# Four of the twelve modulation units move from TensorE to VectorE, and their weights are loaded earlier

## The reference, cut to what matters

```python
mod = jax.nn.silu(c) @ w_ada[l] + b_ada[l]
shift1, scale1, gate1, shift2, scale2, gate2 = jnp.split(mod, N_MOD, axis=-1)
h = modulate(rmsnorm(x, norm1_w[l]), shift1, scale1)      # needs shift1, scale1
...
x = x + gate1[:, None, :] * mix                           # after the mixers
h2 = modulate(rmsnorm(x, norm2_w[l]), shift2, scale2)     # before the experts
...
x = x + gate2[:, None, :] * ffn
```

## Time and profile before

| what | value |
|---|---|
| median of three runs | 918.78 us (916.0 to 918.87) |
| the profiled execution | 919.4 us, of which the span is 917.6 us |
| PE, DVE, ACT, POOL busy | 97%, 45%, 34%, 12% of the span |
| mean rate of the loads | 314 GB/s |
| 0 to 245 us | everything ahead of the experts |

### The profile page before, as it was taken

One profiled execution on the slowest core, in us unless ns is written; L12 is line 12 of the kernel. 1 busy time (PEld: TensorE's weight loads), 2 busy tenths in 40 slices (PEclk: granted clock), 3 DMA queues, 4 the chain that ended last, 5 costly groups with the idle time before them and its releaser, 6 DMA issues.

```text
span 917.6 us, 13421 instructions
## 1 busy us (share of the span) xinstructions
PE 893.3 (97%) x5530; PEld 575.9 (63%) x5530; DVE 410.6 (45%) x697; ACT 314.3 (34%) x507; POOL 106.2 (12%) x116
## 2 busy tenths in 40 slices
PE   5999999999999999999999999999998999999998
PEld 2688876777644434444344444444435899999886
DVE  2357725368522323222223232223234778888643
ACT  1227335342522222322222212222213555555531
POOL 1024463031000000000000000000000022222200
PEclk9999999999999999999999999999999999999999
DMA  9962259787999899999999999999999665555301
GB/s 353 415 291 93 93 193 355 282 326 292 398 402 419 313 420 421 421 419 420 420 421 418 419 421 420 423 419 419 421 421 357 217 194 183 180 179 184 128 1 47
DMA packets 60892, 289.47 MB, mean 315 GB/s; under 512 B 4500, under 2 KB 28692, under 8 KB 33688
## 3 DMA queue, kind: packets, MB, share of 16 engines
q1 hardware_dynamic: 59104, 284.13, 78.3%
q10 hardware_dynamic: 1720, 4.40, 1.2%
HBM read 287.47 MB, written 1.05 MB: 314 GB/s over the span
## 4 chain that ended last, share of the span: by engine, by line
PE 90%; DVE 3%; DMA 3%; issue 2%; ACT 1%; POOL 1%; SPq 0%; ACTq 0%; DVEq 0%
PE ps L1032 24%; PE ps L1056 12%; PE ps L537 8%; PE ps L1020 7%; PE ps L1153 7%; PE ps L1154 7%; PE ps L1155 7%; PE ps L620 4%; PE ps L1072 3%; PE ps L1045 2%; DMA ring<-in_ada_units_dram 2%; PE ps L552 2%; PE ps L520 2%; DMA S<-in_first_cols_dram 1%; PE ps L511 1%
## 5 line engine op out<-in xcount | busy, mean ns | idle before, releaser
L1035 PE MATMUL ps<-ring,proj 128*64 128x512 f32 x320 | 140.9, 593 | 0.0
L1032 PE MATMUL ps<-ring,proj 128*64 128x512 f32 x304 | 133.9, 593 | 0.0
L1853 DVE TENSOR_TENSOR w_l<-ring,w_h 128x2048 fp32r<-128x2048 f32 x33 | 75.5, 2292 | 44.8 <-ACT w_h L2201 44.8
L1153 PE MATMUL ps<-h_h,w_h 128*128 128x256 f32 x336 | 95.1, 283 | 0.0
L1154 PE MATMUL ps<-h_l,w_h 128*128 128x256 f32 x336 | 95.1, 283 | 0.0
L1155 PE MATMUL ps<-h_h,w_l 128*128 128x256 f32 x336 | 95.1, 283 | 0.0
L1032 PEld LDWEIGHTS ps<-ring,proj 128*64 128x64 f32 x304 | 41.1, 137 | 84.6 <-issue 84.6
L1032 PE MATMUL ps<-arena,proj 128*64 128x512 f32 x208 | 91.6, 593 | 0.0
L2201 ACT CAST w_h<-ring 128x2048 fp32r<-128x2048 f32 x33 | 62.8, 1903 | 81.4 <-PE ps L1155 76.9
L1709 DVE SCALAR_TENSOR_TENSOR RQ<-ps,gate_of,proj 128x512 f32<-128x512 f32 x32 | 24.0, 751 | 147.1 <-PE ps L1057 147.1
L2157 ACT CAST MX_r<-RQ 64x512 fp32r<-64x512 f32 x62 | 38.2, 616 | 143.9 <-DVE RQ L1709 143.1
(11 more groups left out here) (372 smaller groups left out, 1601.7 us busy)
## 6 DMA issues: line engine op xcount, KB each, us to landing
ring<-in_w_dram SPq DMA_DIRECT2D x114, 1024.0 KB, 15.0
arena<-in_w_dram SPq DMA_DIRECT2D x72, 1024.0 KB, 15.7
ring<-in_ada_units_dram SPq DMA_DIRECT2D x11, 2048.0 KB, 8.6
ring<-in_ffn_w_in_dram SPq DMA_DIRECT2D x22, 1024.0 KB, 8.1
ring<-in_in_units_dram SPq DMA_DIRECT2D x6, 2048.0 KB, 23.1
ring<-in_ffn_w_out_dram SPq DMA_DIRECT2D x5, 2048.0 KB, 8.0
arena<-in_in_units_dram SPq DMA_DIRECT2D x2, 2048.0 KB, 24.8
ring<-in_out_units_dram SPq DMA_DIRECT2D x2, 2048.0 KB, 9.2
```

Source lines behind the costliest of these rows:

```text
L1032: pe.matmul(ps[0:SLOTS, :], XTe[i % 2][:, k, :], u1[:, k, :], start=(k == 0), stop=(k == 7))
L1035: t = pe.matmul(ps[64:64 + SLOTS, :], XTe[i % 2][:, k, :], u3[:, k, :], start=(k == 0), stop=(k == 7))
L1153: pe.matmul(ps, ah, bh, start=first, stop=False)
L1853: ve.tensor_tensor(low, src, dst.bitcast(F32), ALU.subtract).then_inc(split_ready, 1)
```

## The change

- Units 4 to 7 are no longer made on TensorE. VectorE makes them by a new `ada(j)`: eight instructions over 128 x 512, the first a product of the unit's first 512 columns with a number per partition (`ccol`), the other seven a product with such a number and an addition to the sum so far. Each waits for the one ahead of it. The sum over the partitions is left to the small product on TensorE, now with the constant `ones` in place of `sel`.
- Unit 4 is loaded between units 1 and 0 of the delta projection, and unit 5 between units 0 and 2; before, both came after three `proj` units. VectorE makes them in pieces of two instructions among its convolutions. Units 6 and 7 are made whole, at the ends of VectorE's levels 1 and 2.
- `gate_total(4)` and `(5)` move on TensorE from level 4 to ahead of `project(0)`, and on VectorE from the end of level 3 to ahead of level 1.
- `spread_out` and ScalarE's copies now write contiguously; the stride of eight is in the reading of the weights of `column_total` instead. For segments 3 and 4 (units 6 to 9) eight matmuls with 128 columns of weights take the place of sixteen with 64.
- The slots are dealt out anew: `proj` 0 and 1 now wait for VectorE's units 4 and 5, and later units follow in a rotated order of slots.

```diff
L1256 DVE COPY part<-ps tensor_program
             def gate_total(j, src):
                 ps = take("total", j)
-                pe.wait_ge(*drained("ada", j))
-                pe.matmul(ps[:, :], sel, src, start=True, stop=True).then_inc(*mm.up("total", j))
+                pe.wait_ge(ada_rows, by_vector.index(j) + 1)
+                pe.matmul(ps[:, :], ones, src, start=True, stop=True).then_inc(*mm.up("total", j))
...
             def column_totals(seg):
-                column_total(seg, 1, column_total(seg, 0))
+                ps = take("columns", seg)
+                for half in range(2):
+                    if seg == 3:
+                        pe.wait_ge(ada_rows, by_vector.index(2 * seg + half) + 1)
+                    else:
+                        pe.wait_ge(*drained("ada", 2 * seg + half))
+                for c in range(8):
+                    i = pe.matmul(ps[:, 2 * c:2 * c + 2], by_eights[:, c, :], (ones if seg == 3 else sel)[:, 0:2], start=True, stop=True)
+                i.then_inc(*mm.up("columns", seg, 0))
+                mm.at["columns", seg, 1] = mm.n
...
+            gate_total(4, part[0])
+            gate_total(5, part[1])
             project(0)
             project(1)
...
-                elif level == 5:
-                    ada(7)
                 elif level == 2:
                     project(3)
...
                 elif level == 4:
-                    gate_total(4, part[0])
-                    gate_total(5, part[1])
                     turn_rotated(0)
...
                     project(4)
-                    ada(4)
-                elif level == 3:
-                    ada(5)
                 elif level == 4:
                     turn_rotated(1)
-                    ada(6)
L1256 DVE COPY part<-ps vector_program
+            def ada(j, chunks=range(8)):
+
+                w, dst = unit(("ada", j), 512), part[j % 2]
+                for c in chunks:
+                    if c == 0:
+                        if j in (4, 5):
+                            ve.wait_ge(*mm.of("columns", 1, 1))
+                        else:
+                            ve.wait_ge(*mm.of("total", j - 2))
+                        ve.wait_ge(*filled(("ada", j)))
+                        ve.tensor_scalar(dst, w[:, 0, :], ccol[:, 0:1], None, ALU.mult).then_inc(*vd.up("ada", j))
+                    else:
+                        ve.wait_ge(*vd.of("ada", j))
+                        ve.scalar_tensor_tensor(dst, w[:, c, :], ccol[:, c:c + 1], dst, ALU.mult,
+                                                ALU.add).then_inc(*((ada_rows, 1) if c == 7 else vd.up("ada", j)))
...
-                ve.tensor_copy(by_eights[:, :, 64 * (j % 2):64 * (j % 2) + 64].rearrange("k c p -> k p c"),
-                               full("ada", j)[:, :].rearrange("k (p c) -> k p c", c=8)).then_inc(*free("ada", j))
+                ve.tensor_copy(part[j % 2], full("ada", j)[:, :]).then_inc(*free("ada", j))
...
-            delta_conv(1, range(4))
-            delta_conv(0, range(4))
+            delta_conv(1, range(1))
+            for m in range(1, 4):
+                delta_conv(1, (m,))
+                ada(4, range(2 * m - 2, 2 * m))
+            for m in range(4):
+                delta_conv(0, (m,))
+                ada(4, (6, 7)) if m == 0 else ada(5, range(2 * m - 2, 2 * m))
             ve.tensor_copy(ab_turned, full("ab")[:, 0:256]).then_inc(*free("ab"))
             delta_conv(2, (0,))
+            ada(5, (6, 7))
...
+            gate_total(4)
+            gate_total(5)
             idb = mid(cst("ident_half"), 4)
...
                 if level == 1:
                     lower(3)
+                    ada(6)
                 elif level == 2:
                     lower(5)
-                elif level == 3:
-                    gate_total(4)
-                    gate_total(5)
+                    ada(7)
L1256 DVE COPY part<-ps scalar_program
-                    ada(4)
...
-                    ada(5)
...
-                    ada(6)
                 elif level == 5:
-                    ada(7)
                     higher(6)
L1256 DVE COPY part<-ps sync_program
             load_in("dn", 1, 2560)
+            load_ada(4)
             load_in("dn", 0, 2048)
+            load_ada(5)
             load_in("dn", 2, 3072)
...
             load_in("proj", 1, 512)
-            load_ada(4)
-            load_ada(5)
             load_ada(6)
             load_ada(7)
```

More of the change, by code:

```diff
@@ L289, in program @@
         part = [part_[:, n, :] for n in range(2)]
-        by_eights = part_[:, :, :].rearrange("k a b -> k (a b)").rearrange("k (c p) -> k c p", c=8)
+        by_eights = part_[:, :, :].rearrange("k a b -> k (a b)").rearrange("k (p c) -> k c p", c=8)
         row_high = [v.rearrange("p (k t) -> p k t", k=4) for v in (vrow_r[:, :], gates_r[:, 1, :])]
@@ L409, in program @@
         HIGH, FIFTH = 3, 4
-        for name, s in ((("ada", 0), 0), (("ada", 1), 1), (("ada", 2), 2), (("ada", 3), HIGH), (("dn", 1), R + 1), (("dn", 0), R),
-                        (("dn", 2), FIFTH), (("proj", 2), 0), (("proj", 0), 1), (("proj", 1), 2), (("ada", 4), FIFTH), (("ada", 5), 0),
-                        (("ada", 6), 1), (("ada", 7), FIFTH), (("proj", 3), 2), (("ada", 10), 0), (("ada", 8), 1), (("ada", 9), FIFTH),
-                        (("proj", 4), 0), (("ada", 11), 2), (("wo", 0), 1), (("wo", 1), FIFTH)):
+        for name, s in ((("ada", 0), 0), (("ada", 1), 1), (("ada", 2), 2), (("ada", 3), HIGH), (("dn", 1), R + 1), (("ada", 4), 0),
+                        (("dn", 0), R), (("ada", 5), 1), (("dn", 2), FIFTH), (("proj", 2), 2), (("proj", 0), 0), (("proj", 1), 1),
+                        (("ada", 6), FIFTH), (("ada", 7), 2), (("proj", 3), 0), (("ada", 10), FIFTH), (("ada", 8), 1), (("ada", 9), 2),
+                        (("proj", 4), FIFTH), (("ada", 11), 0), (("wo", 0), 1), (("wo", 1), 2)):
             units.place(name, s)
@@ L434, in program @@
         for i, name in enumerate(moe_order):
-            units.place(name, (2, 0, 5, 6, 7, 1, FIFTH, HIGH)[i % (R + 3)])
+            units.place(name, (0, FIFTH, 5, 6, 7, 1, 2, HIGH)[i % (R + 3)])
         units.place(("mixer",), 1, 2)
         for i, name in enumerate([("fin", u) for u in range(11)] + [("fout", u) for u in range(6)]):
-            units.place(name, (FIFTH, HIGH, 2, 0, 1)[i % R], 2 if name[0] == "fin" else 1)
+            units.place(name, (2, HIGH, 0, FIFTH, 1)[i % R], 2 if name[0] == "fin" else 1)
         first_a, first_b, second_in = sem("first_down_a"), sem("first_down_b"), sem("second_down")
@@ L476, in program @@
         chunk_ready_a, chunk_ready_v = sem("chunk_ready_a"), sem("chunk_ready_v")
-        diagonal_ready = sem("diagonal_ready")
+        diagonal_ready, ada_rows = sem("diagonal_ready"), sem("ada_rows")
+        by_vector = (4, 5, 6, 7)
         rows_made, gated, router_scaled, h2_rows = (sem(n) for n in ("rows_made", "gated", "router_scaled", "h2_rows"))
@@ L794, in tensor_program @@
                     ada(10)
-                else:
+                elif level == 6:
                     project(7)
@@ L1910, in ada @@
                 ps, dst = full("ada", j), part[j % 2]
-                if j in (6, 7):
-                    ac.wait_ge(*mm.of("total", 4))
-                    ac.wait_ge(*mm.of("total", 5))
-                elif j in (4, 5, 8, 9):
-                    ac.wait_ge(*mm.of("columns", {4: 1, 8: 3}[j - j % 2], 1))
+                if j in (8, 9):
+                    ac.wait_ge(*mm.of("columns", 3, 1))
                 elif j > 9:
                     dst = late_part[j % 2]
-                if j in (6, 7, 8, 9):
-                    half = slice(64 * (j % 2), 64 * (j % 2) + 64)
-                    ac.copy(by_eights[:, :, half].rearrange("k c p -> k p c"),
-                            ps[:, :].rearrange("k (p c) -> k p c", c=8)).then_inc(*free("ada", j))
-                else:
-                    ac.copy(dst, ps[:, :]).then_inc(*free("ada", j))
+                ac.copy(dst, ps[:, :]).then_inc(*free("ada", j))
             ac.wait_ge(*vd.of("scale1"))
@@ L2411, in used @@
                 if kind == "ada":
-                    return mm.of("ada", i)
+                    return (ada_rows, by_vector.index(i) + 1) if i in by_vector else mm.of("ada", i)
                 if kind == "dn":
```

## The result

The changed kernel takes 931.25 us, the median of four runs (928.9 to 935.13), beside 918.83 for the kernel before (916.0 to 918.89). The ratio is 1.0141, with an interval of 1.0101 to 1.0182. The forecast was 917.6 us with a range of 913.8 to 920.4, so it had the sign wrong and the range too narrow. The profiled execution took 929.36 us, its span 927.6, 10.0 us more than before.

The account below looks back on a forecast made before the run. TensorE was taken as the bound, busy 893.3 of 917.6 us, with GpSimd deciding at level 4's end. Terms -1.9 + 1.0 - 0.1 - 0.2 gave -1.2: 918.2 us profiled, 917.6 as median, range 913.8 to 920.4.

Parts of the forecast that it names:

- The columns: Contiguous `spread_out` writes and eight 128-column matmuls in `column_totals`: 0.1 us won at the start, 0.2 in all.
- TensorE's clock: One fall from 2.4 to 1.2 GHz expected among the level 5 waits, costing 1.0 us (bounds 0 and 1.9).
- The gate totals: Moved ahead of `project(0)`, they take 1.8 us there; a 0.23 us wait goes, so what follows is 1.6 later.
- Units 4 and 5: On VectorE between convolutions: 5.0 us a unit, 1.3 a pair, fitting its idle time; cost taken as 0.
- Unit 6: On VectorE behind `lower(3)`: 5.0 us fits the 5.87 idle ahead of `lower(4)`; cost 0.
- Unit 7: Behind `lower(5)`, taking turns with GpSimd: `rotate(1, 0)` begins at 137.8 us for 135.21, level 5's mask ready at 147.8.
- Levels 4 and 5: TensorE waits 2.9 us for the last rotated half, 1.0 for the mask, 0.9 for the copy; -1.9 at level 5's `xm`.
- The sum: All terms for the whole kernel: -1.9 + 1.0 - 0.1 - 0.2 = -1.2 us.
- The rival on the slow side: Long waits at level 4's end bring the clock down twice or longer, a turn costs 0.69: +2, 920.8 us; chance 0.11.
- the third case: Rival: GpSimd isn't held up by unit 7, level 5's mask at 145.3: -4.8 us, 914.0; chance 0.17.

Follow-up runs that it names:

- the doubled groups: Kernel before, with its sixteen contiguous small matmuls of `column_totals` for segments 3 and 4 each sent twice over: 922.26 us, ratio 1.0055.

## Why the prediction was wrong

*The columns* is the step that failed: a term of the sum that was put at almost nothing. "with 128 columns of weights they take 0.23 each (...), so eight are again 1.8." The price was read from a row whose weights are read contiguously, and the new reading has a stride of eight. With it the eight take 3.7 us, and 2.08 for 1.06 at the start. The step counted the stride where it was taken away, in VectorE's copies (1.04 to 0.69 us), and not where it went. (The copies wrote their numbers 128 floats apart, in runs of eight numbers; the stride of eight floats is the reader's.) The step forecast -0.3 us, 0.1 for the copies and 0.2 for the groups. The reading costs +1.3 at the first delta matmul (1.7 in the kernel with it alone) and +3.8 at the two `column_totals`, 5 to 5.5 us, and with the clock behind it the layout costs +13.7. The Trainium skill states the rule that was not weighed (Advanced Engine Details and Errata, SBUF Cachelines): reads that land on a different 16-byte line each time pay a penalty. Eight floats are two such lines; the rows agree, 216 ns for 138.

*TensorE's clock* is the second step that failed. One fall at level 5 was forecast at +1.0, and it came: granted clock 0.50 from 150 us on, `xm` 3.64 us for 2.08. The error was to look for falls only where TensorE waits. The falls behind both `column_totals` follow stretches in which it is shown as busy. The kernel with the doubled groups shows that this needs no stride and no wait that the trace shows.

*The gate totals* were forecast at +1.8 less 0.23, "TensorE is without a gap there". Between 35.98 and `xm` of level 0 the changed kernel loses another 4.0 us (104.56 for 99.28, less 1.3): 1.8 are the totals and 2.25 the wait for banks. The step priced the instructions and not the PSUM banks they take in turn; with the totals behind `project(1)` the wait was gone.

*Units 4 and 5* at 0 were right. Each instruction takes 0.75 to 0.78 us for the 0.65 assumed, a pair 1.53 for 1.3, and VectorE's copy at 73.13 still has 0.31 us of idle time ahead. No wait of TensorE came, and units 4 and 5 alone are faster than before.

*Unit 6* was right: 5.96 us for 5.0, with 0.31 left ahead of `lower(4)`.

*Unit 7.* The turns came as forecast, but their effect on TensorE did not. Unit 7 took 8.9 us beside GpSimd, where unit 6 alone took 6.0, but `rotate(1, 0)` began 3.35 later than before when TensorE was 3.1 later, so it was hardly held up. The prediction put all of the turns on GpSimd's path; but the trace of before already had 4.38 us of waiting for ScalarE ahead of that rotation, and the turns went into it.

*Levels 4 and 5* went better than forecast until the clock fell. The waits were 1.11, 0.95 and 0.89 us for 2.9, 1.0 and 0.9, and from `xm` of level 3 to `xm` of level 5 the changed kernel won 3.1 us, where 1.6 was forecast (from -0.3 to -1.9). Then 1.6 went to the fall by the first scores, for 1.0. From `xm` of level 3 to the first step of level 6 it is 0.9 us shorter in all, with 5.6 of units and 1.8 of totals taken out.

*The sum.* The change without the layout's part is 12.4 - 13.7 = -1.3 us, near the -1.2 forecast. That is no support for it: the two numbers come from different groups of runs, the interval of the change alone is 3.7 us to either side, and the bank wait was not in the forecast while the price of the turns was. The agreement is luck. The kernels with all four units and no strided weight read are slower than before (+8.1 and +5.1), so no way was found in which units 6 and 7 pay. *The rival on the slow side* named the clock, but at the end of level 4, and had 2 us of the 12. Two slips in the sums change nothing: by its rows `lower(5)` would end at 126.9 us (122.59 + 2.69 + 1.6), not 127.1, and the third case is 914.0 where it is worked out and 913.8 in the range.

What stays open: the runs that weren't profiled show by their mean clock how much the falls cost, but not where they are. What in a stretch of thin matmuls brings the clock down, its length or the number of matmuls, isn't shown either, since the doubled groups change both. Nor was the change run with the layout mended for units 0 to 3 alone.

## What to carry to other kernels

When a change moves a stride from a copy to a reader, price the reader: look whether the row you take the price from reads its memory in the same steps. Count a stretch of thin matmuls as a risk to the clock as if it were a wait, and look at what stands behind it. Compare the mean granted clock of the runs before you explain a difference by instructions: here it tells most of the loss. And before two more users go into a rotation of buffers, list who gets which buffer behind them; a unit whose result is needed as a row can move, one needed as a column brought a strided access along in every kernel here.

## What the runs showed of the hardware

- A weight load of 64 float32 columns takes 138 ns contiguous and 216 with a stride of eight floats; of 128 columns, 191 and 333. One load with its matmul of two columns goes from 0.11 to 0.23 us for 128 columns of weights (1.77 and 3.74 us for sixteen).
- VectorE's product-and-add over 128 x 512 from SBUF takes 0.78 us contiguous, 1.26 with one input at a stride of eight floats, and 1.18 with the output and the sum at a stride of 128 floats.
- Matmuls with two columns each, 3.2 us of them in a row with contiguous weights and 3.7 with strided ones, all shown as busy, were followed by a granted clock of 0.50. 1.75 us of them were not, in any profiled run.
- Over a whole run the clock prices itself: the kernel before takes 915.0 to 915.9 us at a mean granted clock of 1.000 and 916.7 to 918.1 at 0.996 to 0.998.
- VectorE and GpSimd take turns on SBUF operands: seven product-and-adds take 7.98 us beside GpSimd, 1.11 each, and 5.48 alone, and four of GpSimd's 5.83 beside them, for 2.79 alone.
